# Key norm of a recurrent stage: logarithm and exponential on ScalarE in place of square root and reciprocal

## The reference

```
kk = heads(k * k_k)                                   # 8 heads of 64
kk = kk * lax.rsqrt(jnp.maximum(jnp.sum(kk * kk, axis=-1, keepdims=True), 1e-12))
```

```
s_kk = einsum('bhvk,bhk->bhv', s, kk_t)
s = s * w_t - s_kk[..., None] * (kk_t * a_t) + v_t[..., None] * k_t
```

## Time and profile before

| | us |
|---|---|
| three timed runs | 3726.36, 3729.82, 3731.13 |
| their median | 3729.82 |
| the profiled execution, own time | 3726.41 |
| span of its instructions | 3724.8 |
| key norm, first product to last copy | 2524.1 to 2558.0 |
| first matmul of the recurrence | 2559.05 |

### The profile page before, as it was taken

One profiled execution on the slowest core, in us unless ns is written; L12 is line 12 of the kernel. 1 busy time (PEld: TensorE's weight loads), 2 busy tenths in 40 slices (PEclk: granted clock), 3 DMA queues, 4 the chain that ended last, 5 costly groups with the idle time before them and its releaser, 6 DMA issues.

```text
span 3724.8 us, 57679 instructions
## 1 busy us (share of the span) xinstructions
PE 3232.9 (87%) x22992; PEld 2406.0 (65%) x22992; DVE 1733.0 (47%) x2566; ACT 1327.2 (36%) x1747; POOL 760.9 (20%) x438
## 2 busy tenths in 40 slices
PE   7999988868774999899999899995778779689996
PEld 5877555543331688688772587774777657468885
DVE  3110245555888533311101611435677441469996
ACT  4331233442223332244221322222222132268884
POOL 3444100000000444344430222101111144200001
PEclk9999999978887999999999998556899879889998
DMA  2222511101110122122227212000000012289997
GB/s 105 96 91 89 203 40 45 45 23 48 53 58 32 65 93 96 68 96 91 90 94 277 71 57 79 23 0 10 4 4 4 3 67 92 103 336 412 412 411 277
DMA packets 106920, 397.13 MB, mean 107 GB/s; under 512 B 11680, under 2 KB 11696, under 8 KB 106240
## 3 DMA queue, kind: packets, MB, share of 16 engines
q1 hardware_dynamic: 95040, 347.42, 25.1%
q0 software_dynamic: 8400, 35.15, 2.5%
q10 hardware_dynamic: 3312, 12.06, 0.8%
HBM read 361.55 MB, written 33.03 MB: 106 GB/s over the span
## 4 chain that ended last, share of the span: by engine, by line
PE 75%; DVE 16%; issue 3%; ACT 2%; DMA 2%; POOL 1%; DVEq 1%; ACTq 0%; SPq 0%; POOLq 0%
PE psum L221 12%; PE psum L220 12%; PE psum L222 12%; PE psum L1714 6%; DVE mem L867 5%; PE psum L514 5%; PE psum L2570 3%; PE psum L2571 3%; PE psum L2572 3%; PE psum L1383 2%; PE psum L1064 2%; PE psum L522 2%; PE psum L1363 2%; PE psum L1744 1%; PE psum L545 1%
## 5 line engine op out<-in xcount | busy, mean ns | idle before, releaser
L210 POOL TENSOR_TENSOR ring_r<-ring,whi 128x1024 fp32r<-128x1024 f32 x247 | 594.6, 2418 | 999.2 <-ACT whi L205 999.2
L205 ACT ACTIVATE whi<-ring 128x1024 fp32r<-128x1024 f32 x247 | 255.7, 1055 | 530.7 <-DMA ring<-stream 530.4
L222 PE MATMUL psum<-xn_r,whi 128*128 128x512 f32 x1024 | 406.7, 397 | 0.0
L1714 PE MATMUL psum<-mem 64*64 64x64 f32 x9664 | 265.9, 235 | 85.8 <-DVE mem L2029 61.2
L1714 PEld LDWEIGHTS psum<-mem 64*64 64x64 f32 x9664 | 251.7, 149 | 100.0 <-DVE mem L2029 68.3
L2507 DVE TENSOR_TENSOR er_r<-er,eh 128x1024 fp32r<-128x1024 f32 x268 | 310.0, 1218 | 1.5 <-ACT eh L2495 0.8
L753 PE MATMUL psum<-xn,ring 128*128 128x512 f32 x512 | 238.2, 629 | 69.0 <-ACT mem L792 64.6
L220 PE MATMUL psum<-ffn_xh,ring_r 128*128 128x512 f32 x704 | 280.0, 398 | 18.4 <-DVE xn_r L233 18.4
L2495 ACT ACTIVATE eh<-er 128x1024 fp32r<-128x1024 f32 x268 | 268.9, 1070 | 45.1 <-DMA er<-experts 44.2
L221 PE MATMUL psum<-ffn_xh,whi 128*128 128x512 f32 x704 | 281.5, 400 | 0.0
L753 PEld LDWEIGHTS psum<-xn,ring 128*128 128x128 f32 x512 | 103.1, 203 | 204.1 <-issue 198.9
(11 more groups left out here) (506 smaller groups left out, 6180.8 us busy)
## 6 DMA issues: line engine op xcount, KB each, us to landing
ring<-stream SPq DMA_DIRECT2D x359, 512.0 KB, 3.5
er<-experts SPq DMA_DIRECT2D x276, 512.0 KB, 8.4
xs_dram<-zero_row POOLq DMA_DIRECT2D x1, 12288.0 KB, 38.5
xs<-xs_dram SPq DMA_DIRECT2D x23, 512.0 KB, 8.4
ys_dram<-y_t ACTq DMA_DIRECT2D x23, 512.0 KB, 6.7
mem<-rpb POOLq DMA_DIRECT2D x8, 512.0 KB, 4.3
resid<-x_t SPq DMA_DIRECT2D x1, 2048.0 KB, 8.3
spill<-resid POOLq DMA_DIRECT2D x1, 2048.0 KB, 10.2
```

The source lines that it names most:

```text
L205: act.activation(WHI.get(part, whi)[:, (SLAB_AT[part] + j) % RING, :, :], w, ACT.Copy).then_inc(w_hi, 1)
L210: pool.tensor_tensor(ring_r[:, s, :, :], ring[:, s, :, :], f(WHI.get(part, whi)[:, s, :, :]), ALU.subtract).then_inc(w_lo, 1)
L222: return pe.matmul(bank, hi[:, b, :], x_lo_, start=False, stop=stop, skip_group_check=True)
L1714: ins = pe.matmul(psum[o, bank, n * L:(n + 1) * L], lhs(n)[r], rhs(n)[r], start=i == 0 if start is None else start, stop=i == len(terms) - ...
```

## The change

The square root of the clamped sum becomes its natural logarithm, and an exponential with scale -0.5 follows on ACT, so that knt holds the sum to the power -1/2. The four reciprocals of DVE are gone, and the multiply by knt now waits for the exponential. The names of the steps follow (l0 to l3 new, i0 to i3 gone). Nothing else is edited; from L1613 on the lines move by 3, and from L1942 on they have their old numbers again.

```diff
--- before.py
+++ after.py
@@ -1546,8 +1546,8 @@
         dve_l = Marks("rwkv_dve_levels", lambda c: [f"{n}{l}" for l in LV for n in (("ym", "x", "xt") if l < 5 else ("ym", "xt"))])
         dve_s = Marks("rwkv_dve_state", lambda c: (("z", "zz") if c + 1 < NCH else ()) + (("y0", "y1") if second_sum(c) else ()))
         pool_p = Marks("rwkv_pool_decay", lambda c: ("tb0", "tb1", "kap0", "kap1") + (("rho0", "rho1") if emits(c) else ()))
-        kn_act = Steps(sem("keynorm_act"), "s0 s1 s2 s3 r0 r1 r2 r3")
-        kn_dve = Steps(sem("keynorm_dve"), "k0 k1 k2 k3 m0 m1 m2 m3 n0 n1 n2 n3 i0 i1 i2 i3 f0 f1 f2 f3 w0 w1 w2 w3")
+        kn_act = Steps(sem("keynorm_act"), "s0 s1 s2 s3 l0 l1 l2 l3 r0 r1 r2 r3")
+        kn_dve = Steps(sem("keynorm_dve"), "k0 k1 k2 k3 m0 m1 m2 m3 n0 n1 n2 n3 f0 f1 f2 f3 w0 w1 w2 w3")
         kn_pe = sem("keynorm_pe")
         rz = sem("rwkv_zeros")
         lora_in = sem("lora_in")
@@ -1609,7 +1609,10 @@
                 act.activation(knt[:, t, :], kkn[:, t, :], ACT.Square).then_inc(s, 1)
             for t in range(4):
                 act.wait_ge(kn_dve.sem, kn_dve.at(0, f"n{t}"))
-                act.activation(knt[:, t, :], knt[:, t, :], ACT.Sqrt).then_inc(s, 1)
+                act.activation(knt[:, t, :], knt[:, t, :], ACT.Ln).then_inc(s, 1)
+            for t in range(4):
+                act.wait_ge(s, kn_act.at(0, f"l{t}"))
+                act.activation(knt[:, t, :], knt[:, t, :], ACT.Exp, scale=-0.5).then_inc(s, 1)
             act.wait_ge(kn_dve.sem, kn_dve.end(1))
 
             def sigmoid_in(c, d):
@@ -1936,9 +1939,6 @@
                 dve.tensor_scalar(knt[:, t, T:TA], psum[:, 2 * t + 1, 0:TC], 1e-12, None, ALU.max).then_inc(s, 1)
             for t in range(4):
                 dve.wait_ge(kn_act.sem, kn_act.at(0, f"r{t}"))
-                dve.reciprocal(knt[:, t, :], knt[:, t, :]).then_inc(s, 1)
-            for t in range(4):
-                W(f"i{t}")
                 dve.tensor_tensor(kkn[:, t, :], kkn[:, t, :], knt[:, t, :], ALU.mult).then_inc(s, 1)
             for d in range(2):
                 dve.tensor_copy(wab[:, d, 0:4], col("w0", 4 * d, 4)).then_inc(s, 1)
```

## The result

| | before | changed |
|---|---|---|
| four runs each, median us | 3728.09 | 3706.07 |
| lowest and highest | 3722.76, 3731.13 | 3700.85, 3713.33 |
| ratio of the two, 95% interval | | 0.9944 [0.9923, 0.9965] |
| profiled execution, own time | 3726.41 | 3713.33 |

A forecast was written before the change was run, and what follows sets the result against it. The prediction took TensorE as busy 87% and carrying 75% of the chain, but DVE's reciprocals as bare at the key norm. Replacing them gave -14.96 us: 3729.82 - 14.96 = 3714.9 us, range 3708.5 to 3721.

The forecast's parts named there:

- The path through the key norm: Key norm: four bare DVE reciprocals (19.30 us) go, the first multiply waits for the first exponential instead; 14.96 us earlier.
- Its terms: Key norm: 828 ns per logarithm or exponential, a table load of 1.28 us, DVE idle about 4.3 us before the multiplies.
- the level: Whole kernel: new runs were taken to lie at 3729.82 us, the median of three timed runs, before subtracting 14.96.
- the clock: TensorE's granted clock in the recurrence: nothing counted for it in the sum, +-3 us allowed in the range.
- the first bursts: Start of the recurrence: TensorE's first matmuls again slow, 3.66 us for 16 of L1744 against 1.93 at full clock.
- theory B: Follow-up theory, recurrence: what ran before fixes the clock's pattern; sharpened, clock changes come at instants fixed from the attention's end.
- The prediction's price: From 2559 to 3000 us: each microsecond more at TensorE's low clock level costs about 0.32 us.
- The size of the scatter: Whole kernel: level of the runs, own time against median with spread 4.8, gives +-3.5 us below, a little less above.
- The clock took nothing of the gain: First rival, recurrence: shifted low-clock stretches eat half the gain, about 3722 us; chance 0.08.
- the recurrence did not stay at the low level: Second rival, recurrence: long stretches at low clock make it slower, up to about 3819 us; chance 0.03.
- the load was met: Third rival, key norm: no table load needed between logarithm and exponential, -16.2 us, about 3713.6; chance 0.02.
- the logarithms were as fast as roots: Fourth rival, key norm: logarithms or exponentials much slower than roots; at twice the length about 3719 us; chance 0.03.

## Why the prediction was right and wrong

- **The path through the key norm** was right: the reciprocals were bare, the first exponential is late in their place, no other wait came up. 14.96 us were forecast, 14.75 found; the multiplies took 3.56 us for 3.49, and TensorE's own matmuls there 0.1 us more.
- **Its terms** were right: 828 ns for a logarithm or exponential of 128x768 (3.04 us for four), 1283 ns for the load, 5.2 us from the first logarithm to the first multiply (5.23), DVE idle 4.3 us (4.27), 11.2 us between L1700's and L1744's like (2537.51 to 2548.76: 11.25). The 1.4 us of drain that the Trainium skill names ("ScalarE: Activation LUTs", What ACT_TABLE_LOAD costs) are not seen: the load starts 0.02 us after the last logarithm ends and the exponential 0.02 us after its load ends. The Trainium skill (same page, Table sets: the hidden batching unit) has a single load for logarithm and exponential; this program's trace has one ahead of each.
- **The steps that failed** are two terms of the sum, not the path. 3706.07 lies 8.8 us under the forecast 3714.9. One term is the level, "I take the median's level as that of new runs": 3729.82, the median of three, is 3.0 us above the mean of all 61 runs, 3726.8. The other is the clock, "I count nothing for this": the gain is 18.8 us where 14.96 were forecast, 3.8 more. I had noted that the first bursts are slow again, which they are (3.66 us), and treated all behind them as +-3 us without a sign. It has a sign in the first five chunks, 2.5 to 2.8 us less in each of the three pairs of traces, 2.6 in the mean; the other 1.2 us are within the +-2.4 and have no cause shown. The last 2.0 us are the draw of the four runs, their median 3706.1 against the mean 3708.1 of all 16, and so luck.
- **What the clock did** is not that its steps stand at fixed instants behind the attention's end, as theory B's sharper wording had it: the rise in the recurrence came 56.1 to 56.6 us behind it before, 39.2 to 39.8 with the change, and 42.5 to 43.0 with one or two multiplies more. What is shown is that it repeats while the program stays the same and moves, by another amount than the start does, when the start is moved. The prediction's price for it held: some 10 us less at the low level went with 2.6 us less time. Over the 441 us from the first L1744 on, the mean clock is 0.87 before and 0.88 with the change, a low share of about 26% against about 24%, so the whole of that stretch did not part far from what the prediction assumed.
- **The size of the scatter** was put too small: +-3.5 us from three runs that spread over 4.8, where 61 runs of the same kernel spread over 17.8 (3718.3 to 3736.1). So the low end, 3708.5, was cut too close; the mean of all runs of the changed kernel, 3708.1, lies 0.4 us under it and their median, 3709.1, above it.
- **The rivals**: none came true. The clock took nothing of the gain but added to it, the recurrence did not stay at the low level, the load was met, the logarithms were as fast as roots.

What stays open: what sets the instants at which the clock rises and falls, why the traces of before agree on the first 90 us and part later (407.1 to 413.9 for the whole recurrence), whether the 2.6 us are still there at the recurrence's end, and whether a later stage too has a share that goes with the edit.

## What to carry to other kernels

A reciprocal on a wide tile is worth replacing where it stands bare on the chain: here 4.9 us for 128x768 against 0.83 us for an ACTIVATE, and even with a table load that nothing hides, three quarters of it came off the end. Behind such a place don't take the clock as noise only: compare two traces of one program at a fixed marker, and if they agree to 0.2 us there, a shift of the start can change that stage too, in either direction: here the 90 us behind the key norm lost 2.6 us by the edit and gained 0.7 to 2.7 by smaller shifts. Where a gain is only a few times the scatter of single runs, a handful of runs gives its sign, not its size.

## What the runs showed of the hardware that was not expected

- The granted clock's rises and falls repeat from run to run relative to the program: a rise 4.9 to 5.4 us behind the attention's end and the next 56.1 to 56.6, in three executions of the kernel before that had reached that point up to 2 us apart.
- One multiply of 0.9 us more on VectorE cost 2.7 us more on the stage behind (first to fifth tanh 91.8 against 89.1, in one trace), with a rise of the clock about 3 us later.
- Keeping TensorE busy through an idle gap of 11 us held the clock at 1.00 up to its end and made the next 16 matmuls 1.7 us faster, and no gain was left in the means (3709.7 against 3708.1 us). The clock was low again from 2546.9 us on, as those 16 ended, with no idle time over 0.98 us since the filled gap.
